# Weight halves of the next stage made ahead, in buffers that three stages share; tile turns placed ahead of late loads

## The reference, cut to what matters

```python
def peer_ffn(h, w_q, sub_keys, down, up):          # the experts, once per layer
        q = (xb @ w_q).reshape(n, PEER_HEADS, 2, PEER_DHALF)
        s = jnp.einsum('thpk,pnk->thpn', q, sub_keys).astype(jnp.float32)
        s_top, i_top = lax.top_k(s, PEER_TOPK)
        ...
        u = jnp.take(down, idx, axis=0)
        act = jax.nn.gelu(jnp.einsum('thkd,td->thk', u, xb))
        v = jnp.take(up, idx, axis=0)
        return jnp.einsum('thk,thkd->td', (gate * act).astype(v.dtype), v)

    return rms_norm(x, final_g)                    # end of the first model

def swiglu(h, w_gate, w_up, w_down):               # feed-forward of the second
    return (jax.nn.silu(h @ w_gate) * (h @ w_up)) @ w_down
```

## Time and profile before

| what | value |
|---|---|
| median of 3 runs | 2722.47 us (2718.2 to 2725.76) |
| profiled execution, its own time | 2720.89 us |
| its span in the trace | 2719.1 us |
| PE, DVE, ACT, POOL busy | 88%, 69%, 45%, 23% |
| mean granted TensorE clock | 0.962 |

### The profile page before, as it was taken

The page is one execution under the profiler, slowest core; times in us unless marked ns, Lnnn a source line. Parts: engine busy times, 40 slices in busy tenths (PEclk is TensorE's granted clock), DMA queues, the critical chain, the costliest instruction groups (busy, mean ns, idle before and its releaser), DMA issues. The chain is left out here.

```text
span 2719.1 us, 35148 instructions
## 1 busy us (share of the span) xinstructions
PE 2382.7 (88%) x12882; PEld 1587.3 (58%) x12882; DVE 1863.2 (69%) x3462; ACT 1219.0 (45%) x2588; POOL 625.9 (23%) x529
## 2 busy tenths in 40 slices
PE   6988788888888988788888879999999998977999
PEld 4774333333334444343332268898888887866887
DVE  4667866677667876867765556676666666798665
ACT  3433434444445544444434354456445445535443
POOL 0003445554444444455444300000000000000000
PEclk8989999999999999999999989999999998977999
DMA  9689999999999999999999935542555554212553
GB/s 390 244 337 409 403 427 426 427 427 421 425 407 422 381 426 423 427 427 427 427 423 427 402 127 186 187 163 97 174 188 179 186 186 165 102 49 110 175 187 118
DMA packets 121706, 811.27 MB, mean 298 GB/s; under 512 B 15713, under 2 KB 18825, under 8 KB 26584
## 3 DMA queue, kind: packets, MB, share of 16 engines
q0 software_dynamic: 74160, 540.05, 47.5%
q1 hardware_dynamic: 47400, 269.32, 27.4%
HBM read 807.12 MB, written 1.15 MB: 297 GB/s over the span
## 5 line engine op out<-in xcount | busy, mean ns | idle before, releaser
L1400 PE MATMUL bank<-rows,diag 128*128 128x512 f32 (+1 forms) x2060 | 993.6, 619 | 215.4 <-ACT diag L1558 214.9
L1792 DVE CUSTOM_DVE_ANT_0 rows<-rows,h 128x1024 f32<-128x1024 f32 (+1 forms) x512 | 620.5, 1224 | 361.8 <-DMA rows<-in_peer_rows,idx 356.2
L1400 PEld LDWEIGHTS bank<-rows,diag 128*128 128x128 f32 (+1 forms) x2060 | 370.6, 194 | 741.8 <-ACT diag L1558 426.6
L1277 POOL DMA_INDIRECT rows<-in_peer_rows,idx x512 | 612.1, 1195 | 738.5 <-PE bank L1400 681.3
L2131 PE MATMUL bank<-hT_pair,high 128*128 128x512 f32 x1408 | 502.2, 400 | 5.6 <-DVE hT_pair L2009 2.7
L2065 DVE TENSOR_TENSOR low<-weight_ring,high 128x2048 fp32r<-128x2048 f32 x148 | 338.5, 2289 | 166.4 <-ACT high L2060 166.3
L2132 PE MATMUL bank<-hT_pair,low 128*128 128x256 f32 x1408 | 396.1, 281 | 0.0
L1549 ACT ACTIVATE picks<-picks 128x1 f32<-128x1 f32 (+1 forms) x512 | 103.4, 202 | 641.9 <-DVE picks L1792 623.0
L2060 ACT CAST high<-weight_ring 128x2048 fp32r<-128x2048 f32 x148 | 282.2, 1909 | 142.8 <-PE bank L2140 112.1
L2131 PEld LDWEIGHTS bank<-hT_pair,high 128*128 128x128 f32 x1408 | 265.6, 189 | 73.3 <-DVE hT_pair L2009 3.9
L2132 PEld LDWEIGHTS bank<-hT_pair,low 128*128 128x128 f32 x1408 | 267.0, 190 | 1.6
(11 more groups left out here) (547 smaller groups left out, 3281.8 us busy)
## 6 DMA issues: line engine op xcount, KB each, us to landing
weight_ring<-in_ffn_w_gate SPq DMA_DIRECT2D x44, 1024.0 KB, 4.7
weight_ring<-in_ffn_w_up SPq DMA_DIRECT2D x44, 1024.0 KB, 4.8
weight_ring<-in_ffn_w_down SPq DMA_DIRECT2D x44, 1024.0 KB, 4.8
mod_ring<-in_mod_w SPq DMA_DIRECT2D x16, 1024.0 KB, 6.5
weight_ring<-in_peer_w_q SPq DMA_DIRECT2D x16, 1024.0 KB, 10.0
half_ring<-in_mod_w SPq DMA_DIRECT2D x24, 512.0 KB, 7.3
rows<-in_mod_w SPq DMA_DIRECT2D x12, 1024.0 KB, 10.3
weight_ring<-in_attn_w_in SPq DMA_DIRECT2D x12, 1024.0 KB, 4.7
```

Of the source, the lines that this page charges most:

```text
L1277: nc.gpsimd.indirect_dma_start(ring[:, s], None, dram["peer_rows"], bass.IndirectOffsetOnAxis(ap=idx[:, T, n:n + 1], axis=0)).then_inc(row ...
L1400: mm = nc.tensor.matmul(bank[:, :], diag[0:n, j % DIAG_SLOTS], ring[0:n, j % ROW_SLOTS, D + half * 512:D + (half + 1) * 512], start=(j in ...
L1792: dotted.up(nc.vector.tensor_tensor_reduce(out=ring[r, s, 0:D], in0=ring[r, s, 0:D], in1=its_h, scale=1.0, scalar=0.0, op0=ALU.mult, op1=A ...
```

## The change

1. Two buffers of 16 KB per partition, each a high and a low half, are allocated ahead of everything else and handed to `first_block`, `experts` and `second_block_start` in place of buffers of their own. A third pair of the feed-forward stays its own.
2. At the end of `first_block` ACT and DVE make one more block, query 0 of the experts; DVE's halves of output blocks now stand behind the modulation sums of the same turn. `make_high(0)` and `make_low(0)` leave the start of `experts`.
3. At the start of `experts` PE turns both tiles first, then multiplies late rows 0 and 1; late row 2 moves behind `score(0)`.
4. In the last 17 slots of the row loop ACT copies and DVE subtracts blocks 0 and 1 of the feed-forward. They leave the start of `second_block_start`.
5. There the high and low halves of block 2 move from ahead of the first root mean square to behind it, and turn pieces 2 and 3 move from ahead of k = 4 to ahead of k = 1.

```diff
# first_block, ACT and DVE
-                for b in (1, 2, 3):
+                for b in (1, 2, 3, 4):
                     make_high(nb + b)
...
                     add_gated(j)
-                    if j + 2 < no:
-                        make_low(nb + j + 2)
                     if j == 2:
                         rows.add(dve, 4)
                         rows.add_sum(dve, 2)
+                    if j + 2 < no + 1:
+                        make_low(nb + j + 2)
# experts
+    b_next = b1 + PH
+    NEXT_HIGH_AT, NEXT_LOW_AT = (total - 17, total - 9), (total - 15, total - 7)
...
-                if j == 1:
-                    late_rows(0, 1)
-            late_rows(1, 3)
+            late_rows(0, 2)
...
             score(0)
-            late_rows(3, late)
+            late_rows(2, late)
...
-            make_high(0)
...
+                if j in NEXT_HIGH_AT:
+                    i = NEXT_HIGH_AT.index(j)
+                    W.wait(act, b_next + i)
+                    act.wait_ge(W.multiplied, b_next)
+                    nc.scalar.copy((w_high, x_high)[i], W.ring[:, (b_next + i) % SLOTS, :]).then_inc(high_made.sem, 1)
...
-            make_low(0)
...
+                if j in NEXT_LOW_AT:
+                    i = NEXT_LOW_AT.index(j)
+                    dve.wait_ge(high_made.sem, hm0 + len(split_block) + i + 1)
+                    dve.wait_ge(W.multiplied, b_next)
+                    nc.vector.tensor_tensor((w_low, x_low)[i], W.ring[:, (b_next + i) % SLOTS, :], (w_high, x_high)[i].bitcast(F32),
+                                            ALU.subtract).then_inc(split.sem, 1)
# second_block_start
-                layers[0].multiply(pe, {0: (0, 1), 4: (2, 3)})
+                layers[0].multiply(pe, {0: (0, 1), 1: (2, 3)})
...
-                layers[0].make_high(act, 0)
                 act.wait_ge(made.sem, m0 + 1)
                 turns[0].make_high(act, range(KD))
-                layers[0].make_high(act, 1)
-                layers[0].make_high(act, 2)
                 for T in range(NT):
                     kit.act(nc.scalar.activation(junk, x[:, T], ACT.Square, accum_out=ss[:, 0, T:T + 1]))
                 nc.scalar.activation(ss[:, 1], ss[:, 0], ACT.Sqrt, scale=1.0 / D, bias=kit.eps).then_inc(rooted.sem, 1)
+                layers[0].make_high(act, 2)
...
-                layers[0].make_low(dve, 0)
                 turns[0].make_low(dve, range(KD))
-                layers[0].make_low(dve, 1)
-                layers[0].make_low(dve, 2)
                 dve.wait_ge(rooted.sem, r0 + 1)
...
                     nc.vector.scalar_tensor_tensor(out=x[:, T], in0=x[:, T], scalar=ss[:, 2, T:T + 1], in1=row,
                                                    op0=ALU.mult, op1=ALU.mult).then_inc(normed.sem, 1)
+                layers[0].make_low(dve, 2)
                 turns[0].invert(dve, by=ss[:, 2])
# build
+    with kit.sb("halves_a", [P, 2, 2048], F32R) as halves_a, kit.sb("halves_b", [P, 2, 2048], F32R) as halves_b:
+        shared = (halves_a, halves_b)
```

More of the change, by code:

```diff
@@ L565, in opening, with first_block @@
     W.used += nb
-def first_block(kit, dram, rows, vec, bias):
+def first_block(kit, dram, rows, vec, bias, shared):
     nc, W, x = kit.nc, kit.weights, kit.x
@@ L582, in first_block @@
         x_hi, x_lo = sb("x_high", [P, KD, SEQ], F32R), sb("x_low", [P, KD, SEQ], F32R)
-        w_hi, w_lo = sb("high", [P, 2, 2048], F32R), sb("low", [P, 2, 2048], F32R)
+        w_hi, w_lo = ([a[:, i] for a in reversed(shared)] for i in range(2))
         shift_scale, gains = sb("shift_scale", [P, 2, KD, 2]), sb("gains", [P, KD, 2])
-        opening(kit, dram, rows, bias, proj[:, :, 0:D], hcT, x_hi, x_lo, vec[:, 2], shift_scale, gains, (w_hi[:, 0], w_lo[:, 0]))
+        opening(kit, dram, rows, bias, proj[:, :, 0:D], hcT, x_hi, x_lo, vec[:, 2], shift_scale, gains, (w_hi[0], w_lo[0]))
         ws_low, bs, sink = sb("ws", [P, 4, P]), sb("bs", [P, GROUPS]), sb("sink", [P, HEADS])
@@ L1075, in _, with experts @@
                         rows.add_sum(dve, 2)
+                    if j + 2 < no + 1:
+                        make_low(nb + j + 2)
         W.used += nb + no
-def experts(kit, dram, rows, vec, late_bias):
+def experts(kit, dram, rows, vec, late_bias, shared):
     nc, W = kit.nc, kit.weights
@@ L1153, in experts @@
     J = GROUP_HEADS
[L1155 to L1157 removed]
+    with kit.sb("rows", [P, ROW_SLOTS, 2 * D]) as ring, kit.sb("keysT", [P, 2, P]) as keysT, \
             kit.sb("scores", [P, NT, 2, NKEYS]) as sc, kit.sb("ranks", [P, 6, 64]) as small, \
@@ L1161, in experts @@
             kit.sb("row_stage", [P, 512]) as row_stage, nc.Block() as block:
+        w_high, w_low = (shared[0][:, i] for i in range(2))
+        x_high, x_low = (shared[1][:, i] for i in range(2))
+        x_hi, x_lo = (a.rearrange("p (t k n) -> p t k n", t=NT, k=KD) for a in (x_high, x_low))
         late_line = vec[:, 1].rearrange("p (v n) -> p v n", n=BLK)[:, 0:len(rows.LATE), :]
@@ L1967, in block @@
     def block(self, kit, g):
[L1968 removed]
+        return kit.weights.ring[:, g % SLOTS, :], self.high[g % SPLIT_SLOTS], self.low[g % SPLIT_SLOTS]
 class Turn:
@@ L2285, in add, with halves_of @@
                                                        scalar=self.halves.half[:, T:T + 1], in1=xs, op0=ALU.mult, op1=ALU.add)
-def halves_of(kit, stack):
+def halves_of(kit, stack, shared=()):
     sb = lambda *a: stack.enter_context(kit.sb(*a))
-    return Halves(kit, sb("hT_pair", [P, KD, 2 * SEQ], F32R), sb("high", [P, SPLIT_SLOTS, 2048], F32R), sb("low", [P, SPLIT_SLOTS, 2048], F32R),
+    pairs = list(shared) + [sb("halves", [P, 2, 2048], F32R) for _ in range(SPLIT_SLOTS - len(shared))]
+    high, low = ([pairs[(i - kit.weights.used) % SPLIT_SLOTS][:, part] for i in range(SPLIT_SLOTS)] for part in range(2))
+    return Halves(kit, sb("hT_pair", [P, KD, 2 * SEQ], F32R), high, low,
                   sb("factors", [P, 4, NT]), sb("wide_factor", [P, SEQ])[:], sb("spread_factor", [P, NT, P]))
@@ L2666, in second_block_start @@
     with contextlib.ExitStack() as stack:
-        halves = halves_of(kit, stack)
+        halves = halves_of(kit, stack, shared)
         work = stack.enter_context(kit.sb("work", [P, 2048]))[:]
```

43 lines of the change are left out of this document (20 added, 23 removed).

## The result

The changed kernel takes 2705.99 us (median of 5 runs, 2704.99 to 2708.19), the kernel before 2721.20 in the same session (2718.20 to 2725.76). The ratio is 0.9941 with a 95% interval of 0.9927 to 0.9955: 15.2 us less, where 10.8 was forecast. The profiled execution of the changed kernel took 2708.19 us, its span 2706.4, so the pair of profiles differs by 12.7 us of span. The 12.7 can be placed. The other 2.5 are a matter of which executions are compared: the profiled execution of the changed kernel is the slowest of its five, 2.2 above their median, and that of the kernel before lies 0.3 under its own.

The account below looks back on a forecast made before the run. DMA engines were taken to bound the experts, PE the feed-forward, with nothing full between. Terms 0.6 + 0 + 0 + 10.2 = 10.8 us, from the median 2722.47, gave 2711.7 us; range 2706 to 2718.

Parts of the forecast that it names:

- First block's end, cost 0: First block's end: query 0's halves fit into DVE's idle 3.25 us with 0.95 to spare; cost 0, without cover up to 2.3.
- Experts' start, 0.6: Experts' start: query starts 1.5 us sooner, late rows from 3 on 0.6 sooner; 0.6 us gained, ends 0 and 1.8.
- Row loop's end, 0: Row loop's end: delays from the four large operations are caught up before the last rows; cost 0, ends 0 and 1.05.
- Feed-forward's start, 10.2: Feed-forward's start: with PE's waits gone, the second gate product starts at 1590.9 instead of 1601.15; 10.2 us gained, ends 5 and 13.
- the stretch of low clock: Feed-forward's start: first turns run at the lower clock, which was let rise at 1581 instead of late in the 1585th us.
- two k at 1.32 us and five at 0.71: Gate block 0 at the feed-forward's start: two k at the lower clock, five at the upper, 2.3 + 3.5 us, ending at 1584.7.
- the rival that it becomes the bound: Feed-forward's start: the factor chain, 0.3 us to spare, comes 3 us later; gain 7.8, time 2714.7; chance 0.15.
- The rest of the first feed-forward, counted as 0: Behind the second gate product: PE is the bound and nothing waits for a fixed time, so no gain was added.
- The rival that half would be given back there: First feed-forward: ACT and DVE fall behind over its first blocks, half the gain is given back; 2717 us; chance 0.11.
- The clock doesn't fall: Feed-forward's start: the 3.2 us pause doesn't lower PE's clock; gain 13.0, time 2709.5 us; chance 0.16.
- Gathers run slower: Experts' row loop: rows land at other addresses, 2% slower gathers cost 25 us, 2737; chance 0.06 with other such losses.
- What would show it: Timeline signs: first turn within 0.5 us of experts' end, second gate product 18 to 19 behind, no PE idle over 0.5 before up block 0.

Follow-up runs that it names:

- number 9: Changed kernel with the experts' late rows back in their old places, all else kept; 2709.72 us, ratio 0.9943 to the kernel before.
- number 1: Kernel before plus shared buffers and only the feed-forward part (halves made ahead in the row loop, new order), old experts' start; 2711.72 us, ratio 0.9955.
- number 10: Changed kernel with each of the four large copies and subtractions in the row loop made twice; 2708.76 us, ratio 0.9934 to the kernel before.
- number 6: Changed kernel with block 2's halves back ahead of the first root mean square; 2709.59 us, ratio 0.9961 to the kernel before.
- number 11: Changed kernel with block 2's halves between the first and second four turned pieces, no filling matmuls; 2708.81 us, ratio 0.9939 to the kernel before.
- number 4: Changed kernel plus five filling matmuls on PE behind the experts' last row; 2710.57 us, ratio 0.9954 to the kernel before.
- number 5: Changed kernel with turn pieces 2 and 3 back ahead of k = 4; 2713.52 us, ratio 0.9965 to the kernel before.
- number 7: Changed kernel with halves of feed-forward blocks 0 and 1 made at the feed-forward's start, new order kept; 2714.99 us, ratio 0.9975 to the kernel before.
- number 2: Kernel before plus shared buffers and only the start part (query 0's halves early, both tiles turned before late rows); 2721.09 us, ratio 0.9993.
- number 8: Changed kernel plus two filling matmuls and block 2's halves between the two groups of turned pieces; 2705.08 us, ratio 0.9940 to the kernel before.

## Why the prediction was right or wrong

The direction and the place were right; the gain was called 10.8 us and is 15.2 by the medians, 12.7 in the pair of profiles. By its own steps:

- *First block's end, cost 0*: right. DVE's idle time before the fourth block's result is 1.04 us, predicted 0.95, so the subtraction went into the wait. The block's end itself moves too much to judge by: 189.85 after, 190.35 and 192.61 in the two traces of before.
- *Experts' start, 0.6*: the steps came true, the size is open. Tile 1 was turned at 197.48 (predicted 197.9), the query started at 202.00 (203.2), row 8 came 3.68 behind row 7. The 0.62 us at the experts' end in the pair of profiles looks like a hit, but it is luck: 0.50 of it was already there at the first block's end, to which I had given no gain. Over all traces the part is worth about 1.3 us at the 33rd dot product (number 9). From the first block's end to the experts' end the three traces without it (before twice, number 1) take 1383.5 us on average, the ten with the whole of it 1382.5: 1.0 us, inside the spread of either group (1381.6 to 1386.0, 1380.4 to 1385.7). Counted from the start of the span the difference is 2.0 us (1574.1 and 1572.1), but half of that already stands at the first block's end, which moves from 188.0 to 194.0 among the ten. The Trainium skill (DMA: Bandwidth & Descriptors, Issuing engines are not separate DMA queues) says that both queues share the 16 engines. From 1100 to 1150 us before, the gathers' queue took 96.0% of the engines' time and SP's 5.0%, together the 1.01 of the earlier trace rows, which agrees. The hole at 216 us says nothing of it, since only SP's queue moved data there (84.4% before, 100.1% after).
- *Row loop's end, 0*: right, shown by number 10.
- *Feed-forward's start, 10.2*: the mechanism was right, the term mis-sized: 11.1 measured, and 11.0 to 11.1 in the five traces with this part unchanged (the changed kernel twice, numbers 1, 9 and 10). The step that failed is the stretch of low clock. I had it low from 1572.1 to 1581, for 8.9 us and over the first turn; it was low for 6.8 us, from 1.8 to 8.6 us behind the experts' end, so the first turn took 1.06 us and not 1.97. All of PE's later work there stands 0.6 to 0.9 us sooner than I had it, counted from the experts' end: first product at 2.98 (3.66), k = 1 at 5.99 (6.9), up block 0 at 12.1 (12.7), second gate product at 18.0 (18.9). That the clock fell late is not what pays. In numbers 6 and 11 the clock fell 0.3 and 0.9 us behind that end, the first turn took 1.94 and 1.62 us, and up block 0 still started at 11.9, for the clock rose sooner as well, at 7.1 and 7.7. It is the length of the low stretch that I had wrong. One sum of mine is off too: two k at 1.32 us and five at 0.71 make 6.2, not 5.8; they took 6.1. The factor's chain ended 0.6 us ahead of PE where I had it 0.3 ahead: the rival that it becomes the bound was near, and numbers 4, 5, 6 and 7 show it as a wait of 0.5, 1.1, 1.4 and 1.4 us as soon as one of the edits is undone or PE made faster.
- *The rest of the first feed-forward, counted as 0*: wrong by 0.7 to 0.9 us. 171.1 in both traces of before, 170.2 to 170.7 in ten with the new order of the feed-forward, though 171.1 in number 6. Number 2, with the old order, has 172.1, with a second stretch of low clock in it. Lined up product by product, before against after, 0.53 of the 0.94 us stand at one place, 17 us behind the second gate product: a wait of 0.25 us for a low half, and slower products right behind it. The wait is gone in the changed kernel and back in number 6, so it hangs on where block 2's halves are made. Another 0.2 stand ahead of that place and 0.2 are spread behind it, for which I have no cause. The rival that half would be given back there is refuted: a little is gained.
- *The clock doesn't fall*: it fell, but later and for a shorter time than I had it. Numbers 4 and 8 priced it: 1.8 and 1.4 us (1.6 less the 0.2 of number 11), where I had 2.2.
- *Gathers run slower*: refuted. The last 40 dot products start within 95.67 us in both kernels, one row each 2.45 us.
- *What would show it*: the signs came true but for two. The first turn stood 0.55 us behind the experts' end, where I had allowed 0.5, and PE sat idle 1.37 us ahead of its first product, where I had allowed 0.5 up to up block 0.

So of the 4.4 us that were missing from the gain, 0.9 is the low clock at the feed-forward's start and 0.9 in this pair the stretch behind it, that I had put at nothing. The other 2.5 are not in the pair of profiles at all: 2.2 because the profiled execution of the changed kernel was its slowest, 0.3 because that of the kernel before was a little under its median. The time itself came out 5.7 us under the forecast, the further 1.3 because I started from 2722.47, the median of three, and the median of the session became 2721.20. Where in the program those 2.2 us lie, no trace shows. That it is the experts is suggested by their taking 1381.5 and 1383.3 us in two traces of the same kernel. That the start part is worth more than I gave it would need the kernels with both parts whole (the changed one twice, numbers 10 and 11, ratios 0.9934 to 0.9947) to stand clear of the feed-forward part alone (0.9955). Their intervals overlap, and number 9, with half of the start part undone, has 0.9943. Whether that part brings nothing or a few us, these runs can't settle.

## What to carry to other kernels

Where two stages meet and nothing is full, list the operations between the last result of one and the first full rate of the other, and ask of each whether its inputs existed earlier: here two copies and two subtractions did, and the last rows of a stage bound by its transfers had room for them twice over. Once the waits are gone, the order of small work inside the join (turns early under the first products, a chain's own work ahead of what serves later) was worth 4.4 (undone one at a time) to 4.7 of 11 us. A saturated stage upstream doesn't pass on a lead unchanged, and a change's gain there can't be read from one pair of traces: take a second trace of each kernel before believing a difference of half a per mille, and compare the granted clock of the two, stretch by stretch, before blaming an engine.

## What the runs showed of the hardware

The clock's fall isn't tied to PE's pause alone. In all traces with the halves made ahead and without fillers PE stood idle for 3.13 us before the first turn. In the changed kernel (twice) and in numbers 1, 9 and 10 the turn of 8 then took 1.06 us, in number 11 1.62, in number 5 1.88 and in number 6 1.94: the fall came 1.6 to 2.1 us behind the experts' end, 0.9, 0.6 and 0.3. In the kernel before it came at 0.1 and 0.0, and in number 7, with the same idle PE, at 2.4. The Trainium skill (TensorE: Matmul & The Clock Gate, Part 1: The HAM clock gate) says that the watch runs freely of the kernel; the traces agree. It moves PE by up to 0.9 us at that turn alone, but not in the end: the clock was low for 6.8 us in all eight of these traces, whenever it fell, and up block 0 came at 11.9 in numbers 6 and 11, no later than in the changed kernel (12.1). It was low for 13.7 us before (twice) and for 10.2 in numbers 2 and 7; in these four PE came back to work 4.4 us later. In number 2, where this stretch is as in the kernel before, the clock was at 0.77 some 12 us behind the experts' end (1582 to 1583) and full behind it, where in the kernel before it was at 0.61 some 13.5 us behind (1585 to 1586). So f1 was 28.24 there and not 29.16.

A filler that multiplies 128 x 128 by 128 x 512 in plain f32 took 0.9 us at the upper clock, where the products of 128 x 512 on halves take 0.39 by the same kind of record: five fillers hold PE for 4.5 us.

A distance of tens of us repeats within one kernel to 0.1 us (f1), a long stage doesn't. From the first block's end to the experts' end it took 1380.4 to 1386.0 us in fourteen traces, with nearly the same instructions. A part of that is the granted clock. Some 820 us behind the first block's end PE makes the 20 products shown above. In five traces (before twice, numbers 2, 5 and 6) the clock was low there for 3.4 us, and from the first of them to the query's first took 9.7 to 10.0 us. In the other nine it was low for 6.8 us, and they took 10.8 to 11.3. The stage lasts 1381.7 us on average in the five and 1383.4 in the nine; the changed kernel is among the nine in both its traces, the kernel before among the five. Whether the change has a part in which of the two comes up, these traces don't tell: numbers 2, 5 and 6 hold parts of it and are among the five.

Later stages, which the change doesn't touch, follow the clock too. From the first feed-forward's sum to the next sum into x it is 119.0 to 119.5 us in the three traces in which the clock was not low there at all, 120.2 to 120.8 in the four with 3.4 us of low clock, 121.2 to 121.4 in the six with 6.8, and 123.6 in number 8 with 10.2. Another stage takes 428.0 to 428.9 us in the nine traces with 78 to 85 us of low clock in it (before 428.1, after 428.3), and 429.6 to 433.7 in the five with 92 to 96 (number 4 433.7, number 8 430.3). In these two stages number 8, the kernel with the shortest start of the feed-forward, lost 2.2 and 2.0 us against the changed kernel in the profiled execution, more than the 1.6 it had won. That is why these medians resolve no gain of that size.
